# The projection stage of a decoder layer: tiles written out one by one, w_in products placed between the small PE steps of the tile before

## The reference, cut to what matters

```python
def rms_norm(x, g):
    xf = x.astype(jnp.float32)
    y = xf * lax.rsqrt(jnp.mean(xf * xf, axis=-1, keepdims=True) + EPS)
    return (y * g.astype(jnp.float32)).astype(x.dtype)

# h = rms_norm(x); P = h @ w_in, 1720 columns: c_q 256, c_kv 128, k_rope 32, q 512,
# six k/v groups of 128, gates 24
q = (rms_norm(cq, g_cq) @ w_uq).reshape(B, S, H, MLA_NOPE + MLA_ROPE)      # H = 8, 64 + 32
kv = (rms_norm(ckv, g_ckv) @ w_ukv).reshape(B, S, H, MLA_NOPE + MLA_V)     # 64 + 64
k_nope, v = kv[..., :MLA_NOPE], kv[..., MLA_NOPE:]
k = jnp.concatenate([k_nope, jnp.broadcast_to(krope[:, :, None, :], (B, S, H, MLA_ROPE))], axis=-1)
q = rms_norm(q, g_q)
k = rms_norm(k, g_k)
# then rotary position on the last 32 of q and k
# the other group: rms_norm of its 8 q heads and of two of its k groups; sigmoid of the gates
```

## Time and profile of before

| | |
|---|---|
| three runs: median, lowest, highest | 3569.02, 3564.1, 3569.88 us |
| the profiled execution | 3564.53 us |
| span, first to last instruction | 3562.9 us |
| mean granted clock of TensorE over the span | 0.916 |
| PE busy | 3011.3 us, 85% of the span |
| DVE busy | 1207.1 us, 34% |
| ACT busy | 609.0 us, 17% |
| products with w_in (L428), x512 | 187.4 us busy |

### The profile page before, as it was taken

The page is one execution under the profiler, slowest core; times in us unless marked ns, Lnnn a source line. Parts: engine busy times, 40 slices in busy tenths (PEclk is TensorE's granted clock), DMA queues, the critical chain, the costliest instruction groups (busy, mean ns, idle before and its releaser), DMA issues.

```text
span 3562.9 us, 47319 instructions
## 1 busy us (share of the span) xinstructions
PE 3011.3 (85%) x15924; PEld 2200.9 (62%) x15925; DVE 1207.1 (34%) x3431; ACT 609.0 (17%) x1547; POOL 182.9 (5%) x188
## 2 busy tenths in 40 slices
PE   3477756999997996599999999999999998999990
PEld 1244436666664654487777777777876786777770
DVE  1155440677772563222122222222222221222224
ACT  0011110555551331010000000100110010000100
POOL 0000000000000011000000000000000000000000
PEclk8788875999998995799999999999999999999995
DMA  2512122533003100766544576566876564645835
GB/s 103 192 51 51 39 61 55 151 80 80 13 2 95 54 26 16 263 238 213 175 171 157 201 275 211 199 237 219 280 271 225 203 236 164 241 156 181 290 114 243
DMA packets 306094, 555.15 MB, mean 156 GB/s; under 512 B 80350, under 2 KB 115422, under 8 KB 304840
## 3 DMA queue, kind: packets, MB, share of 16 engines
q1 hardware_dynamic: 265912, 509.39, 42.3%
q0 software_dynamic: 21152, 38.50, 3.1%
q10 hardware_dynamic: 18832, 4.33, 0.6%
HBM read 525.89 MB, written 70.93 MB: 168 GB/s over the span
## 4 chain that ended last, share of the span: by engine, by line
PE 52%; issue 3%; DVE 2%; DVEq 1%; DMA 1%; ACT 1%; ACTq 1%; POOL 0%; POOLq 0%
PE ps L1641 34%; PE ps L1659 16%; PE ps L1664 2%; DVE x L1610 1%; PE ps L1623 1%; ACT xT_e L1527 0%; DMA d_ys<-ys_e,dst 0%; ACTq L1427 0%; DVE gg L1578 0%; DVEq L1427 0%; DVEq L1430 0%; DMA xg<-d_h,src 0%; DVE ys_e L1595 0%; DVEq L1563 0%; ACT ss L1546 0%
## 5 line engine op out<-in xcount | busy, mean ns | idle before, releaser
L1641 PE MATMUL ps<-xT_e,wg 128*128 128x128 f32 (+2 forms) x8192 | 1248.3, 315 | 31.8 <-issue 27.9
L1641 PEld LDWEIGHTS ps<-xT_e,wg 128*128 128x128 f32 x8192 | 1207.6, 197 | 88.2 <-issue 49.1
L1659 PE MATMUL ps<-w_rows,aT 128*128 128x512 f32 x1248 | 567.8, 612 | 11.8 <-issue 10.1
L1659 PEld LDWEIGHTS ps<-w_rows,aT 128*128 128x128 f32 x1248 | 239.2, 195 | 321.3 <-issue 321.3
L1578 DVE TENSOR_SCALAR gg<-ps,bias 128x128 f32<-128x128 f32 (+2 forms) x256 | 101.2, 395 | 703.0 <-PE ps L1641 702.9
L1546 ACT ACTIVATE ss<-gg 128x128 f32<-128x128 f32 (+2 forms) x256 | 88.7, 346 | 888.2 <-DVE gg L1578 887.9
L1546 ACT ACT_TABLE_LOAD x32 | 41.1, 1283 | 881.8 <-issue 881.8
L428 PE MATMUL ps<-w_in,hT_a 128*128 128x430 f32 x512 | 187.4, 528 | 0.1
L724 PE MATMUL ps<-ident_t,sc 128*128 128x128 f32 x880 | 149.6, 286 | 31.0 <-ACT sc L790 27.6
L790 ACT ACTIVATE sc<-sc,nm 128x640 f32<-128x640 f32 (+15 forms) x256 | 161.6, 634 | 67.3 <-DVE nm L832 67.3
L1595 DVE COPY ys_e<-ps 128x1024 f32<-128x1024 f32 x22 | 26.3, 1222 | 423.4 <-PE ps L1664 221.3
(11 more groups left out here) (290 smaller groups left out, 2598.8 us busy)
## 6 DMA issues: line engine op xcount, KB each, us to landing
wg<-in_w_gate_up SPq DMA_DIRECT2D x128, 2048.0 KB, 8.1
w_rows<-in_w_down SPq DMA_DIRECT2D x128, 1024.0 KB, 4.9
wg<-d_ys SPq DMA_DIRECT2D x8, 2048.0 KB, 10.9
d_bias<-d_rev SPq DMA_DIRECT2D x1, 10368.0 KB, 40.5
w_in<-in_w_in SPq DMA_DIRECT2D x1, 6880.0 KB
x_a<-in_x POOLq DMA_DIRECT2D x8, 512.0 KB, 8.5
kn<-d_kn SPq DMA_DIRECT2D x8, 512.0 KB
strip_t<-d_bias SPq DMA_DIRECT2D x8, 512.0 KB
```

What stands on the lines that cost most here:

```text
L1641: mm = pe.matmul(ps[:, j % 2, half * PASS:half * PASS + w], wg[:, j // 2, k, c0:c0 + 255:2], xT[:, k, 0:w], start=(k == 0), stop=(k == KD ...
L1659: mm = pe.matmul(ps[:, 2 + 2 * b + h, :], aT[:, j, b * P:b * P + r], wd[:, c, j % 2, h * 512:(h + 1) * 512], start=(j == 0), stop=(j == JD ...
```

## The change

The four loops of two tiles are gone; each engine's work is written out for tiles 0 to 7.
- **PE** has functions for its steps: `turn_x`, `into` (a part of the products: tile, chunk, parts k), `turn_c`, `up`, `turn_n`, `turn_q`. Between the small steps of tile t stand the products of tile t+1: 12 before `turn_c`, 2 before `up`, 6 before `turn_n`, 8 before `turn_q`, 4 after it, and then `turn_x(t+2)`. For tile 7 there are none.
- **DVE** makes `hT` in two halves, each with its own count, ahead of the `pr` copy of the tile in hand; the reciprocal and `xn` of tile t+2 stand between the sums of squares and the rest of tile t.
- **ACT** makes the squares and root of tile t+2 right behind the `pr` copy of tile t; the sigmoid comes behind the root of `st2`, tile by tile.
- **SP** stores `vs` and `vw` as soon as `pr` is there, then `v_m`, gates, the `nT` pieces, and last the two `qkT` pieces. Stores count on `s_st[b]`, one semaphore per parity.
- **POOL** loads x of tile t when `xn` of tile t-2 is made, and the table when `qk` of tile t-2 is made.
- Credits and the chains' loop counts are gone; `s_oT` becomes `s_n` and `s_q`; `x` and `trig` count per parity.

```diff
             @block.gpsimd
             def _(pool):
-                with pool.Fori(0, NT // 2) as u:
...
+                for t in range(0, NT):
+                    b, rows = t % 2, slice(t * P, (t + 1) * P)
+                    if t >= 2:
+                        pool.wait_ge(s_xn, t - 1)
+                    pool.dma_start(x[b][:, :], e.x[0, rows, :]).then_inc(s_x[b], 16)
+                    if t >= 2:
+                        pool.wait_ge(s_qk, t - 1)
+                    pool.dma_start(trig[b][:, :], e.c_trig[rows, :]).then_inc(s_trig[b], 16)
 
             @block.sync
...
+                for t in range(NT):
+                    sp.wait_ge(s_prA, t + 1)
+                    sp.wait_ge(s_prD, t + 1)
...
+                    sp.wait_ge(s_upD, t + 1)
...
+                    sp.wait_ge(s_gt, t + 1)
...
+                    sp.wait_ge(s_nT, t + 1)
...
+                    sp.wait_ge(s_qA, t + 1)
+                    sp.wait_ge(s_qD, t + 1)
+                    sp.dma_start(e.d_qm[:, :, rows].rearrange("h d p -> d h p"), qkT[b][:, 0:HM, :]).then_inc(s_st[b], 16)
+                    sp.dma_start(e.d_km[:, :, rows].rearrange("h d p -> d h p"), qkT[b][:, HM:, :]).then_inc(s_st[b], 16)
+                for b in range(2):
+                    sp.wait_ge(s_st[b], 160 * (NT // 2))
 
             @block.scalar
...
+                spread(0)
+                spread(1)
+                for t in range(NT):
+                    b = t % 2
+                    act.wait_ge(s_pr, t + 1)
+                    if t >= 2:
+                        act.wait_ge(s_st[b], 160 * (t // 2))
+                    act.activation(pr[b][:, 0:2 * PCH].rearrange("p (c n) -> p c n", c=2), ps[:, 4 * b:4 * b + 2, 0:PCH], ACT.Copy).then_inc(s_prA, 1)
+                    if t + 2 < NT:
+                        spread(t + 2)
+                    rest(t)
 
             @block.vector
...
+                def columns_of(t):
+                    b = t % 2
+                    for c in range(2):
+                        dve.wait_ge(s_xT, t + 1)
+                        dve.tensor_tensor(hT[b][:, 4 * c:4 * c + 4, :], ps[:, 4 * b + c, :].rearrange("p (n d) -> p n d", d=P),
+                                          bcast(g_x[:, 4 * c:4 * c + 4].unsqueeze(2), [P, 4, P]), ALU.mult).then_inc(s_hT, 1)
...
+                rows_of(0)
+                rows_of(1)
+                columns_of(0)
+                for t in range(NT):
+                    if t + 1 < NT:
+                        columns_of(t + 1)
+                    spreads(t)
+                    if t + 2 < NT:
+                        rows_of(t + 2)
+                    rest(t)
 
             @block.tensor
...
+                def turn_x(t):
+                    b = t % 2
+                    pe.wait_ge(s_xn, t + 1)
+                    if t >= 2:
+                        pe.wait_ge(s_qA, t - 1)
+                        pe.wait_ge(s_qD, t - 1)
...
+                def into(t, c, ks):
+                    b = t % 2
+                    for k in ks:
+                        if c == 0 and k % 4 == 0:
+                            pe.wait_ge(s_hT, 2 * t + k // 4 + 1)
+                        mm = pe.matmul(ps[:, 4 * b + c, 0:PCH], hT[b][:, k, :], w_in[:, k, c * PCH:(c + 1) * PCH], start=(k == 0), stop=(k == KD - 1))
+                    if c == 3 and ks[-1] == KD - 1:
                         mm.then_inc(s_pr, 1)
...
+                turn_x(0)
+                for c in range(4):
+                    into(0, c, range(KD))
+                turn_x(1)
+                for t in range(NT):
+                    more = t + 1 < NT
+                    if more:
+                        into(t + 1, 0, range(KD))
+                        into(t + 1, 1, range(4))
+                    turn_c(t)
+                    if more:
+                        into(t + 1, 1, range(4, 6))
+                    up(t)
+                    if more:
+                        into(t + 1, 1, range(6, KD))
+                        into(t + 1, 2, range(4))
+                    turn_n(t)
+                    if more:
+                        into(t + 1, 2, range(4, KD))
+                        into(t + 1, 3, range(4))
+                    turn_q(t)
+                    if more:
+                        into(t + 1, 3, range(4, KD))
+                    if t + 2 < NT:
+                        turn_x(t + 2)
```

More of the change, by code:

```diff
@@ L253, in _ @@
                 sp.dma_start(e.d_bias.rearrange("h p n -> p h n"), bass.AP(e.d_rev.tensor, 0, [[0, P], [REV, 2 * (HN + 1)], [1, REV]])).then_inc(e.rev_copied, 16)
[L254 to L276, removed]
@@ L279, in _ @@
+                for b in range(2):
+                    sp.wait_ge(s_st[b], 160 * (NT // 2))
             @block.scalar
             def _(act):
[L281 to L311, removed]
-                    for b in range(2):
-                        t = 2 * u + b
-                        act.wait_ge(s_oT, CREDIT + 4 * u + 1 + b)
-                        act.activation(nT[b][:, :, :].rearrange("p (c n) d -> p c (n d)", c=2), ps[:, 4 * b:4 * b + 2, :], ACT.Copy).then_inc(s_gt, 1)
-                    for b in range(2):
-                        t = 2 * u + b
-                        act.wait_ge(s_oT, CREDIT + 4 * u + 3 + b)
-                        act.activation(qkT[b][:, 0:HM, :].rearrange("p (c n) d -> p c (n d)", c=2), ps[0:QK, 4 * b:4 * b + 2, :], ACT.Copy).then_inc(s_oTA, 1)
-                    ch.end()
@@ new lines, in _ @@
+                act.wait_ge(s_w, 16 * 28)
+                act.wait_ge(s_eps, 1)
+                spread(0)
[9 more added lines that the diff above has]
+                    rest(t)
@@ new lines, in turn_c, with up @@
+                def turn_c(t):
+                    b = t % 2
+                    pe.wait_ge(s_cn, t + 1)
+                    pe.wait_ge(s_prD, t + 1)
+                    for k in range(3):
+                        mm = pe.transpose(ps[:, 4 * b + 3, k * P:(k + 1) * P], cn[b][:, k * P:(k + 1) * P], ident[:, :])
+                    mm.then_inc(s_cT, 1)
+                def up(t):
+                    b = t % 2
+                    pe.wait_ge(s_cTd, t + 1)
+                    pe.wait_ge(s_prA, t + 1)
+                    for c in range(2):
+                        for k in range(2):
+                            pe.matmul(ps[:, 4 * b + c, 0:4 * QK], cT[b][:, k, :], w_uq[:, k, c * 4 * QK:(c + 1) * 4 * QK], start=(k == 0), stop=(k == 1))
+                    for c in range(2):
+                        mm = pe.matmul(ps[:, 4 * b + 2 + c, :], cT[b][:, 2, :], w_ukv[:, c * 512:(c + 1) * 512], start=True, stop=True)
+                    mm.then_inc(s_up, 1)
@@ new lines, in turn_n, with turn_q @@
+                def turn_n(t):
+                    b = t % 2
+                    pe.wait_ge(s_nq, 4 * t + 4)
+                    pe.wait_ge(s_upA, t + 1)
+                    for j in range(8):
+                        src = nq[b][:, j * P:(j + 1) * P] if j < 6 else pr[b][:, C_KC + (j - 6) * P:C_KC + (j - 5) * P]
+                        mm = pe.transpose(ps[:, 4 * b + j // 4, (j % 4) * P:(j % 4 + 1) * P], src, ident[:, :])
+                    mm.then_inc(s_n, 1)
+                def turn_q(t):
+                    b = t % 2
+                    pe.wait_ge(s_qk, t + 1)
+                    pe.wait_ge(s_nT, t + 1)
+                    for j in range(2 * HM):
+                        mm = pe.transpose(ps[0:QK, 4 * b + j // 4, (j % 4) * P:(j % 4 + 1) * P], qk[b][:, j, :], ident[:, :])
+                    mm.then_inc(s_q, 1)
```

261 lines of the change are left out of this document (114 added, 147 removed).

## The result

The changed kernel takes 3437.32 us (median of four runs, 3435.65 to 3451.46) against 3566.56 for the kernel before measured with it: a ratio of 0.9648, 95% interval 0.9619 to 0.9677. That is 129 us faster; 3481 was forecast, and the range ended at 3466.

What follows compares the result with a forecast made beforehand. PE and DVE taking turns in the projection stage was taken as the bound. The last copy 84.3 us earlier and stores 3.6 us shorter gave 87.9 us off the 3569.0 median: 3481 us, range 3466 to 3504.

Steps and rivals of the forecast that it cites:

- What bounds the kernel: Projection stage: no engine is full; PE and DVE take turns, about 47.6 us per tile.
- a microsecond taken from the stage is one taken from the kernel: Everything behind the projection stage waits for its barrier, so the stage's 87.9 us would come off the kernel's time.
- Edits costed at nothing: Semaphores, dropped credits, table loads, store waits and written-out code in the stage: no cost; written-out code 1 us either way.
- Everything after it as long as before: Stages behind the projection: their length would not change in the new profile.
- PE's work and the period: Loop, per tile: 31.2 us of PE's work plus waits of 1.35 and 1.0, a period of 33.6 us.
- The tail: Last tile, without products beside it: 32.2 us of bare steps from 396.2 to 428.4, next stage at 434.7.
- The load of x: POOL's load for tile t+3: lands in 8.5 us, costs nothing; at 12.0 it would be 2.2 us late.
- The clock: PE in the loop: upper level throughout, granted clock near 1.00 from 138 to 396, no hole over 1.4 us.
- Late handoffs: Rival in the loop: late x or slower DVE adds some 2.2 us per period, 13 us, 3494; chance 0.15.
- The lower level for the whole loop: Rival: the loop stays at the lower clock, 63 us per period, 3711; chance 0.04 together with no interleaving.
- a clock that swings: Rival: PE's mean clock stays 0.84 in the loop, 38.2 us per period, 3513; chance 0.06.
- No interleaving: Rival: a semaphore holds the next tile's products, a tile takes 23.1 + 0.9 + 1.0 + 32 us; chance 0.04 with the lower level.

Runs made afterwards that it cites:

- `written_out`: Kernel before with the five loops over pairs of tiles written out, order of work, waits, credits and stores untouched: 3529.54 us, ratio 0.9915.
- `before_pad64`: Kernel before with 64 unneeded transposes (128 instructions) on PE at the start of the experts' stage: 3534.08 us, ratio 0.9912.
- `ahead`: Changed kernel with all 32 products of the next tile before `turn_c` and none among the small steps: 3554.68 us, ratio 0.9982.

## Why the prediction was wrong

**What bounds the kernel, and the step "a microsecond taken from the stage is one taken from the kernel": half right.** Nothing is given back beyond chance, but something is added. The step that failed is "Edits costed at nothing", where written-out code was bounded at 1 us either way. I had asked only what fetching costs inside the stage, and there it costs nothing that shows, as said (the products of a tile run at 0.36 us apart from first to last). I had not asked what a longer program does to the code *behind* it: `written_out` has that effect alone and is 34 us faster, and the filler gives it or takes it away without any change of the projection. Adding it to the sum, 3567 - 88 - 34 = 3445, against 3437 measured; the 8 left are within what medians of four such runs can tell (the interval of the ratio is 10 us either way). The prediction's "7 us either way can be measured" was too narrow for the same reason, and its lower end, 5 us under a median, too: the runs of one kernel lie 16 us apart for the changed kernel, 30 for `before_pad64` and 34 for `ahead`. "Everything after it as long as before" was named in the prediction as a thing to check, and it is what turned out wrong.

**PE's work and the period: right.** Forecast 31.2 of work and 33.6 per period, measured 33.46. The forecast wait in front of `turn_q` was 1.35, measured 0.99; in front of the products 1.0, measured 0.78. Most of the difference is in how the rows count: an idle piece starts at the modelled end of the last matmul, which lies some 0.16 behind its slot (the row of 8 products at 258.26 is 3.05 us long, 8 slots are 2.89). With it the waits are 1.15 and 0.94. No wait at `turn_c` or `up` inside the loop, as forecast.

**The tail: right.** The last `pr` copy starts at 395.19 (forecast 396.2), the last `qkT` copy ends at 427.62 (428.4), the next stage starts at 433.56 (434.7). The weights landed 1.5 earlier than in the sum, so counted from there each is 0.4 to 0.7 later than forecast. Of the 6.3 us from copy to next stage 5.9 were needed. The old row of stores costs 2.5 more here.

**The load of x: no cost, as forecast, though the landing was mis-sized.** I took 8.5 us. The loads, now issued one at a time in the loop and no longer in pairs, land in 3.8 to 11.6 us with a median of 4.2:

```profile
DMA to landing us min/median/max: 3.8/4.2/11.6
```

It is there well before ACT asks, and costs nothing.

**The clock: right.** 1.00 from 138 to 396 us, with holes of 0.8 and 1.0. The Trainium skill (TensorE: Matmul & The Clock Gate, "A second HAM failure mode: psum-queue depth-cycling") tells of a kernel whose clock swung because PE idled briefly between groups; holes of 0.8 and 1.0 us did not do that here. `ahead` shows the other side: behind holes of 9.9 us the lower level is back.

**The rivals.** Late handoffs: none seen. The lower level for the whole loop, or a clock that swings: no. No interleaving: `ahead` shows what the kernel is without it, a stage of 402.6 us from first square to next stage against 390.7; I had priced a tile that isn't interleaved at 57 us, and it takes 47.8, since in `ahead` DVE's first steps of a tile, up to `cn`, still run beside the products of the next.

**What stays open.** Why a place is good. Moving the code by a block leaves the packets and the time nearly as they are (the changed kernel with 0 and 256: 92 and 93; the kernel before with 62 and 318, pass by pass the same in 27 of 32), moving it by part of one changes both, and one pair of the two families agrees when one is shifted by 66 instructions. But which jump misses at which place wasn't worked out, nor why 62 and 318, by which the programs' lengths agree modulo 256, didn't bring the kernel before to the changed kernel's packets. Why `ahead` is 17 us slower by its median than A says is open too. The changed kernel with 256 instructions of filler took 3447.82, 10 above the one without; the filler's own time (first gate product 28.3 us after the stage's start, against 25.6) is 2.7 of them. And 82 to 92 packets come with 2051 to 2075 us: the packets don't give the time by themselves.

## What to carry to other kernels

Products with a fixed order can be dealt out by hand among the steps of a chain: sum the chain between two handoffs, put as many products there as last that long, and the period comes out within 1% of the sum; put the transposes that feed the next tile ahead of the last products, not behind them. When a change makes an engine's program longer or shorter, the code behind it moves too: if a long loop with branches follows, look at the instruction queue's packets and at "issue" waits in that loop before crediting (or blaming) the change, and take several executions: one trace here could be 19 us off. In a kernel with such a loop, a few numbers of filler instructions, tried where the engine waits anyway, are worth the runs.

## What the runs showed of the hardware

PE's instructions come in packets of 16 KB, 256 instructions each: the straight stages need one per 256 (29 in attention), the experts' loop 82 to 115 for the same work, depending on where it lies. The Trainium skill (Runtime: NRT & Kernel Launch, "Instruction fetch mechanics") says that blocks of that size are fetched ahead in order and that a taken branch out of the resident window stalls. The 16 KB packets agree, and so does the hole of 3.62 us with a packet in it; in the holes of 1.35 and 2.23 us no packet comes, and what they are wasn't found out. The traces don't show which instruction PE waited for. The good places took 30 to 34 us off by medians (`before_pad64`, `written_out`) and 30 to 51 of 2100 in the single traces, and some of it isn't stall: PE's busy time for the same 10072 matmuls went from 1924.62 to 1914.54 us when the holes went, at a granted clock of 0.96 and 0.97.
